# Three PSUM banks for turned blocks in a shared-key attention, and where eight broadcast matmuls stand

## The chip, the cores and the metric

The kernel runs on one core of one Trainium2 chip. The metric is the time of one execution in microseconds on that core. An engine of the core works through its own queue in order: PE is the matrix engine (TensorE), DVE is VectorE, ACT is ScalarE, POOL is GpSimd, SP is the queue that issues most transfers. They wait for each other through semaphores. PE writes its results to PSUM, which has 8 banks of 128 x 512 f32, and ACT or DVE copy them out.

## The reference, cut to what matters

One transformer block for 1024 tokens of width 1024: adaLN from a conditioning vector, two attention branches side by side, a gated merge, and a mixture of experts.

```
mod = silu(c) @ w_mod + b_mod            # 6 x 1024 values
sh1, sc1, gt1, sh2, sc2, gt2 = split(mod, 6)
h = modulate(rmsnorm(x, g_mix), sh1, sc1)
x = x + gt1 * token_mixers(h)            # branches A and B
h = modulate(rmsnorm(x, g_ffn), sh2, sc2)
x = x + gt2 * hier_moe(h);  out = rmsnorm(x, g_final)
```

Branch B is attention with 8 heads of 64 and a bias of forget gates. Branch A is attention with 8 query heads of 64 and **one** key and value head, on 256 keys that an indexer chooses for each query. Both are causal over blocks of 128 tokens.

## The kernel before, in words

**Units.** The attention is cut into 64 units, `UNITS[n]`. A unit is a pair of heads and a query block `b` of 128 tokens, so it has b+1 key blocks. Units 0 to 31 (`N_B` = 32) are branch B, four pairs with b from 7 down to 0. Units 32 to 63 are branch A, four pairs with b in the order 7, 0, 6, 1, 5, 2, 4, 3. Loops on PE, ACT and DVE run over n from -3 to 63, all in step (`LEAD` = 3). In this text, step n of branch A does this:

- PE: `scores(n+3)` (called S here, L1120) writes the logits of unit n+3 to banks 0 to 3. It waits for `lg_done`, that is for DVE's pass over the unit before. Then for each group f of two key blocks `turn_p(n, f)` (T, L1131) transposes the probabilities of both heads into bank 4 or 5 in turn, and `values(n, f-1)` (V, L1145) multiplies the group before with the values into bank 6. The last V of the unit closes the step. T waits until ACT has copied the group two before; V waits until ACT has copied its own group, and the first V of a unit waits for `o_done`, DVE's copy of the unit before out of bank 6.
- DVE: `out_a(n-1)` (L1619, that copy), `inverse(n+2)` (L1607), `scaled(n+2)` (L1614, the rows divided by their sums, after which the unit may be turned), `largest(n+3)` (L1600, the pass over the logits: bias, row maximum), and then what `parts[n]` has for this step.
- ACT: `turned(n, f)` (L823, the copy of each turned group to SBUF), then `exps(n+3)` (L810, one for each of the two heads).

A unit of width W has W = 128(b+1) logits a row.

**The eight steps before branch A.** In steps 24 to 31, PE also makes the queries of branch A: `qa_tile(i)` (L1159, i = n-24, 16 matmuls into bank 7), which ACT copies out (L829), DVE rotates (`rope_a`, L1648 to L1651) and PE turns one step later (`qa_turn`, L1167). In these steps DVE also runs the search for the 256 keys and, from step 28 on, `choose` (L1635 to L1639), one long piece a step. From step 30 on DVE's order is rope_a, inverse, scaled, largest, and then `parts[n]`; S of step 30 belongs to unit 33.

**The modulation.** For gt1, sh2, sc2 and gt2, DVE sums eight weighted rows of w_mod in each partition (`mod_sums`, L1379 and seven times L1381 for each of eight halves of 512 columns) while PE makes the first projections (L1015, L1020). Later `modulate(n)` multiplies `ones` with such a half on PE (L1176, into bank 7), which adds over the partitions and leaves the sum in all of them, and DVE adds the broadcast rows of b_mod (`bmb`) and writes it back (L1664). It stands in steps 44 to 51 (`MOD_AT` = 44), between the T's and the last V. `modulate_a2` (L1668) follows in step 51; SP loads the first weights of the next stage (L523 to L526) after it.

**Behind the attention.** From step 56 on ACT and DVE also split the activations into two parts (`high`, L843, and `low`, L1672), and the gate stage on PE begins at L1211.

Of the kernel before, what the change touches and what calls it, by code (L numbers as in the profile page):

```python
# [18 lines left out]
P = 128  # L19
# [58 lines left out]
CHOOSE_AT = {28: 7, 29: 6, 30: 5, 31: 2, 32: 4, 33: 3}  # L78
MOD_AT = N_B + TT + 4

# [14 lines left out]
def qa_turn_at(i):  # L95

    return TURN_AT[N_B - TT + 2 + i] - 1


# [23 lines left out]
def build(nc, x, c, positions, w_mod, b_mod, g_mix, w_in, b_forget, w_out_a, w_out_b, w_out, g_ffn,  # L123
# [11 lines left out]
    with ExitStack() as ctx:  # L135
# [105 lines left out]

        bmb = at(8, 4 * U, [4, D])
        gffn = at(12, U)
# [216 lines left out]
        def _(sp):  # L460
# [15 lines left out]
            sp.wait_ge(modp_ok, 1)  # L476
            for n in range(4, 12):
                if n >= 6:
                    sp.wait_ge(acc_ok, n - 3)
                sp.dma_start(mod2[n % 2], w_mod_v[:, :, n * 512:(n + 1) * 512]).then_inc(mod_in[n % 2], 16)  # L480
# [36 lines left out]
            sp.wait_ge(qa_ps, TT)  # L517
            for q in range(4):
                sp.dma_start(bmb[:, q, :], b_mod[0:1, (2 + q) * D:(3 + q) * D].to_broadcast([P, D])).then_inc(bmb_in, 16)
            sp.dma_start(gffn, g_ffn[0:1, :].to_broadcast([P, D])).then_inc(bmb_in, 16)  # L520
# [82 lines left out]
        def _(pool):  # L603
# [19 lines left out]
            pool.wait_ge(p_in, 64)  # L623
            pool.wait_ge(consts, 3)

            for t in range(TT):
# [91 lines left out]
        def _(act):  # L718
# [99 lines left out]
            def turned(n, f):  # L818
                g, k, keys = GROUP_AT[n] + f, TURN_AT[n] + f, key_groups(n)[f]
                act.wait_ge(t_done, k + 1)  # L820
                if g >= 4:
                    act.wait_ge(pv_done, g - 3)
                act.activation(pT_of(n, g)[:, 0:2 * len(keys) * P], ps[:, 4 + k % 2, 0:2 * len(keys) * P], ACT.Copy).then_inc(pt_copied, 1)  # L823

# [143 lines left out]
        def _(pe):  # L968
# [154 lines left out]
            def turn_p(n, f):  # L1123
                k, keys = TURN_AT[n] + f, key_groups(n)[f]
                if f == 0:
                    pe.wait_ge(n_done, 2 * n + 2)
                if k >= 2:
                    pe.wait_ge(pt_copied, k - 1)
                for i, kb in enumerate(keys):
                    for z in range(2):  # L1130
                        m = pe.transpose(ps[:, 4 + k % 2, (2 * i + z) * P:(2 * i + z + 1) * P], logits(n)[z][:, kb * P:(kb + 1) * P], ident[:])  # L1131
                m.then_inc(t_done, 1)
# [18 lines left out]
            def qa_tile(i):  # L1151
                t = TILES[i]
                if i == 0:
                    pe.wait_ge(wqa_in, 64)
                    pe.wait_ge(pj_out, 6 * PAIRS)
                else:
                    pe.wait_ge(qa_tm, i)
                for kt in range(KT):
# [11 lines left out]
            def modulate(n):  # L1170
                if n == 0:
                    pe.wait_ge(acc_ok, 10)
                    pe.wait_ge(qa_tm, TT)
                else:
                    pe.wait_ge(mbc_ok, n)
                pe.matmul(ps[:, 7, :], ones[:], acc[2 + n // 2][:, (n % 2) * 512:(n % 2 + 1) * 512], start=True, stop=True).then_inc(mbc_ps, 1)  # L1176

            for n in range(-LEAD, N_U):
                if n + LEAD < N_U:
                    scores(n + LEAD)  # L1180
                groups = len(key_groups(n)) if n >= 0 else 0
                for f in range(groups):
                    turn_p(n, f)
# [8 lines left out]
                elif N_B - TT <= n < N_B:  # L1192
                    qa_tile(n - (N_B - TT))
                elif MOD_AT <= n < MOD_AT + 8:
                    modulate(n - MOD_AT)
                if groups:
                    values(n, groups - 1)
            pe.wait_ge(mbc_ok, 9)
            pe.wait_ge(o_done, N_U)
# [167 lines left out]
        def _(dve):  # L1367
# [6 lines left out]
            def mod_sums(n):  # L1374
# [3 lines left out]
                a = acc[n // 2][:, (n % 2) * 512:(n % 2 + 1) * 512]  # L1378
                link(dve.tensor_scalar(a, w[:, 0, :], sil[:, 0:1], None, ALU.mult))  # L1379
                for t in range(1, KT):  # L1380
                    m = dve.scalar_tensor_tensor(a, w[:, t, :], sil[:, t:t + 1], a, ALU.mult, ALU.add)  # L1381
# [277 lines left out]
            def modulate(n):  # L1659
                if n == 0:  # L1660
                    dve.wait_ge(bmb_in, 96)
                half = slice((n % 2) * 512, (n % 2 + 1) * 512)
                dve.wait_ge(mbc_ps, n + 1)
                dve.tensor_tensor(acc[2 + n // 2][:, half], ps[:, 7, :], bmb[:, n // 2, half], ALU.add).then_inc(mbc_ok, 1)  # L1664

            def modulate_a2():
                dve.wait_ge(mbc_ok, 8)
                dve.scalar_tensor_tensor(a2, a2, 1.0, gffn, ALU.add, ALU.mult).then_inc(mbc_ok, 1)  # L1668
# [9 lines left out]

            for n in range(MOD_AT, MOD_AT + 8):
                parts.setdefault(n, []).append(lambda n=n: modulate(n - MOD_AT))  # L1680
            parts[MOD_AT + 7].append(modulate_a2)
            for n in range(N_U - TT + 1, N_U):
                parts.setdefault(n, []).append(lambda n=n: low(n - (N_U - TT) - 1))

            for n in range(-LEAD, N_U):
                todo = parts.get(n, [])
                if n > N_B:
                    out_a(n - 1)
                if N_B - TT < n <= N_B:
                    rope_a(n - (N_B - TT) - 1)  # L1690
                if N_B <= n + LEAD - 1 < N_U:
                    inverse(n + LEAD - 1)
                    scaled(n + LEAD - 1)
                if n + LEAD < N_U:
                    largest(n + LEAD)
# [250 lines left out]
```

## Time and the profile before

| | |
|---|---|
| median of 3 runs | 1812.57 us (1811.67 to 1814.99) |
| the profiled execution | 1821.39 us, its span 1819.3 us |
| PE busy | 1678.1 us, 92% of the span |
| DVE, ACT, POOL busy | 961.7, 496.6, 191.5 us |
| mean granted TensorE clock | 0.970 of full |
| steps 24 to 31 of the attention | about 466 to 556.6 us of the span |
| branch A, to the first matmul of the gate stage | about 562.7 to 704.7 us |

The span is the time from the first to the last instruction. Line numbers are those of the kernel before. A line of a timeline is a run of one engine's instructions; in brackets stands how long the engine was idle before it and for whom it waited. PEld is the load of weights into the array, which overlaps PE. Durations are those of this one execution.

### The profile page before, as it was taken

Reading aid. Unit: us, or ns where it says so; the run is one execution under the profiler, and the core shown is the slowest. Engines: PE = TensorE matmul, PEld = TensorE weight load, DVE = VectorE, ACT = ScalarE, POOL = GpSimd, SP = SyncE. Lnnn points to the kernel's source line nnn. Section 1 sums busy time; section 2 is a strip of 40 time slices with the busy share of each in tenths; the row PEclk is TensorE's granted clock in tenths of the full one; section 3 lists DMA queues with packets and bytes.
Section 4 is the critical chain, followed back from the end, with each engine's and each line's share of the span. In section 5 each row is a group of like instructions: output and inputs, shape, how many; then the busy total and the mean of one; then the engine's idle time right before and its main releaser. Section 6 shows DMA issues by size and latency. Waiting matters only on the chain.

```text
span 1819.3 us, 22907 instructions
## 1 busy us (share of the span) xinstructions
PE 1678.1 (92%) x7928; PEld 857.8 (47%) x7929; DVE 961.7 (53%) x1913; ACT 496.6 (27%) x1020; POOL 191.5 (11%) x371
## 2 busy tenths in 40 slices
PE   6998899999998998999999998499999989999892
PEld 3553456465545555666676455233333333333330
DVE  6675788787887664655555433533333333333323
ACT  4124455353535564110100111011111111111112
POOL 0110000000000000000000000122222212222221
PEclk9999999999999999999999998699999999999996
DMA  9641201100001020122112713889999747999997
GB/s 358 223 155 59 70 24 48 31 29 1 1 1 59 1 70 1 35 52 51 35 35 108 300 59 133 335 334 398 365 339 398 278 127 237 397 401 367 398 398 253
DMA packets 102906, 316.63 MB, mean 174 GB/s; under 512 B 9921, under 2 KB 46825, under 8 KB 78257
## 3 DMA queue, kind: packets, MB, share of 16 engines
q1 hardware_dynamic: 91088, 287.88, 41.3%
q0 software_dynamic: 11744, 27.79, 6.3%
q8 instruction: 44, 0.72, 0.2%
q14 instruction: 30, 0.24, 0.0%
HBM read 289.14 MB, written 26.51 MB: 173 GB/s over the span
## 4 chain that ended last, share of the span: by engine, by line
PE 82%; ACT 5%; DMA 5%; DVE 4%; issue 2%; SPq 1%; POOLq 0%; DVEq 0%; ACTq 0%
PE ps L1296 18%; PE ps L1222 10%; PE ps L1314 9%; PE ps L1211 6%; PE ps L1095 5%; PE ps L1257 5%; PE ps L1120 4%; PE ps L1145 4%; DMA arena<-in_w_e_up_dram 3%; PE ps L1101 3%; PE ps L1015 3%; PE ps L1159 3%; PE ps L1131 2%; ACT arena L823 2%; PE ps L1053 2%
## 5 line engine op out<-in xcount | busy, mean ns | idle before, releaser
L1296 PE MATMUL ps<-arena 128*64 128x512 f32 x1632 | 376.3, 604 | 19.6 <-issue 14.0
L1296 PEld LDWEIGHTS ps<-arena 128*64 128x64 f32 x1632 | 115.5, 138 | 233.4 <-issue 219.5
L1884 DVE COPY arena<-ps 128x256 f32<-128x256 f32 x51 | 21.7, 425 | 383.6 <-ACT arena L931 383.6
L1314 PE MATMUL ps<-arena 128*64 128x512 f32 x816 | 186.4, 599 | 0.6 <-DVE arena L1906 0.6
L1222 PE MATMUL ps<-rounded 128*128 128x512 f32 x768 | 183.3, 398 | 0.0
L1535 DVE TENSOR_SCALAR_CACHE_REDUCE arena<-arena,small 128x384 bf16<-128x384 f32 (+2 forms) x192 | 171.1, 939 | 0.0
L1222 PEld LDWEIGHTS ps<-rounded 128*128 128x128 f32 x768 | 144.3, 188 | 36.5 <-issue 7.7
L710 POOL DMA_INDIRECT sum_rows<-arena,ones x51 | 81.4, 1595 | 434.9 <-DVE arena L1906 424.0
L1145 PE MATMUL ps<-arena 128*64 128x128 f32 x1152 | 96.4, 286 | 23.1 <-ACT arena L823 21.5
L1211 PE MATMUL ps<-arena 128*128 128x512 f32 x256 | 115.6, 606 | 2.2 <-DVEq L1708 2.2
L1257 PE MATMUL ps<-arena 128*128 128x512 f32 x256 | 112.0, 595 | 2.0 <-DMA arena<-in_w_out_dram 2.0
L935 ACT ACTIVATE arena<-ps 128x256 f32<-128x256 f32 x51 | 19.5, 383 | 340.8 <-PE ps L1305 340.8
L1600 DVE CUSTOM_DVE_ANT_0 arena<-ps,arena 128x896 f32<-128x896 f32 (+7 forms) x128 | 91.7, 754 | 36.9 <-PE ps L1120 34.8
L823 ACT ACTIVATE arena<-ps 128x512 f32<-128x512 f32 (+1 forms) x160 | 85.4, 551 | 88.3 <-PE ps L1131 88.2
L1714 DVE RECIPROCAL arena<-arena 128x1024 f32<-128x1024 f32 x16 | 104.8, 6553 | 0.5
L810 ACT ACTIVATE arena<-arena,small 128x896 f32<-128x896 f32 (+7 forms) x128 | 97.8, 768 | 10.0 <-DVE small L1600 9.9
L1314 PEld LDWEIGHTS ps<-arena 128*64 128x64 f32 x816 | 54.2, 136 | 94.0 <-issue 88.0
L1145 PEld LDWEIGHTS ps<-arena 128*64 128x64 f32 x1152 | 59.7, 136 | 70.9 <-ACT arena L823 45.3
L1131 PE MATMUL ps<-ident,arena 128*128 128x128 f32 x576 | 89.1, 287 | 0.0
L1889 DVE RECIPROCAL arena<-arena 128x256 f32<-128x256 f32 x51 | 89.1, 1746 | 0.0
L1120 PE MATMUL ps<-arena 64*128 64x512 f32 (+3 forms) x384 | 80.9, 527 | 7.8 <-DVE small L1600 6.9
L890 ACT ACTIVATE arena<-ps 128x1024 f32<-128x1024 f32 x16 | 16.4, 1023 | 259.1 <-PE ps L1222 259.1
(297 smaller groups left out, 2013.7 us busy)
## 6 DMA issues: line engine op xcount, KB each, us to landing
arena<-in_w_e_gate_dram SPq DMA_DIRECT2D x64, 1024.0 KB, 16.5
arena<-in_w_e_up_dram SPq DMA_DIRECT2D x64, 1024.0 KB, 19.1
arena<-in_w_e_down_dram SPq DMA_DIRECT2D x32, 2048.0 KB, 15.8
arena<-in_w_mod_dram SPq DMA_DIRECT2D x12, 2048.0 KB, 9.6
arena<-in_w_in_dram SPq DMA_DIRECT2D x32, 512.0 KB, 4.4
arena<-in_x_dram SPq DMA_DIRECT2D x16, 512.0 KB, 8.3
sum_rows<-arena SPq DMA_DIRECT2D x9, 512.0 KB, 2.6
arena<-cum_rows SPq DMA_DIRECT2D x8, 512.0 KB, 5.3
```

Of the source, the lines that this page charges most:

```text
L810: act.activation(buf, buf, ACT.Exp, bias=nmax[:, u:u + 1], scale=-1.0, accum_out=rs[:, u:u + 1]).then_inc(p_done, 1)
L823: act.activation(pT_of(n, g)[:, 0:2 * len(keys) * P], ps[:, 4 + k % 2, 0:2 * len(keys) * P], ACT.Copy).then_inc(pt_copied, 1)
L1120: m = pe.matmul(ps[:, 2 * z + a // 512, 0:e - a], q[half, b * P:(b + 1) * P], k[half, a:e], start=True, stop=True)
L1131: m = pe.transpose(ps[:, 4 + k % 2, (2 * i + z) * P:(2 * i + z + 1) * P], logits(n)[z][:, kb * P:(kb + 1) * P], ident[:])
L1145: m = pe.matmul(ps[z * HD:(z + 1) * HD, 6, 0:P], v, pT_of(n, g)[:, (2 * i + z) * P:(2 * i + z + 1) * P], start=kb == 0, stop=kb == b)
L1211: m = pe.matmul(ps[:, 4 * half + 2 + g, :], w[2 + g][:, kt, :], oT[g][kt][:, tok], start=kt == 0, stop=kt == 3)
L1222: m = pe.matmul(ps[:, 4 * half + g, :], a, b, start=kt == 0 and k == 0, stop=kt == KT - 1 and k == 2)
L1257: m = pe.matmul(ps[:, 2 * (t % 2) + n, :], mT[:, kt, t * P:(t + 1) * P], wout[:, kt, n * 512:(n + 1) * 512], start=kt == 0, stop=kt == KT - 1)
L1296: m = pe.matmul(ps[o * TB:(o + 1) * TB, 2, 0:2 * FQ].rearrange("p (j n) -> p j n", j=2), xT[:, k % NX, k // NX * TB:(k // NX + 1) * TB], w ...
L1314: m = pe.matmul(ps[o * TB:(o + 1) * TB, 5, 0:DQ], hidT[:, k % NH_T, k // NH_T * TB:(k // NH_T + 1) * TB], w_dn[c][:, k, o * DQ:(o + 1) * D ...
L1535: chain.up(dve.tensor_scalar(junk[b % 2][:, 0:WB[B0 + b]], scb[b], thr(b), None, op, ALU.add, accum_out=cnt[:, b:b + 1]))
L1714: link(dve.reciprocal(e, e))
```

## The change

It has three parts.

1. In branch A from unit 33 on (`FIRST_OF_THREE`), turned groups go through banks 7, 4 and 5 (or 7, 5, 4) in turn, and V runs two groups behind T. The last V of a unit moves behind the S of the next step. T waits for the copy three groups before. DVE's `out_a(n-1)` moves from the head of the step to behind `scaled(n+2)`, in front of `largest(n+3)`.
2. Bank 7 must therefore be free by then: the eight `modulate` move from steps 44 to 51 to steps 24 to 31, between S and the first T on PE and at the head of `parts[n]` on DVE. They share bank 7 with qa_tile: `modulate(i)` waits until ACT has copied tile i-1, and `qa_tile(i)` waits for DVE's copy of half i (`mbc_ok`). `modulate_a2` stands in step 44, and so do the weights that wait for it.
3. b_mod is in the sums from the start: POOL clears four 1024-column tiles (`at(45, 4 * U)`), SP loads the row of b_mod into partition 0 of them, and `mod_sums` adds to that, so that its first instruction is a scalar_tensor_tensor too. The four broadcasts of b_mod fall away, and DVE's part of `modulate` becomes a copy.

```diff
@@ the order of banks
-MOD_AT = N_B + TT + 4
+MOD_AT = N_B - TT
+A2_AT = N_B + TT + 4
+FIRST_OF_THREE = N_B + 1
+def turn_bank(k):
+    k -= TURN_AT[FIRST_OF_THREE]
+    return (7, 4 + TURN_AT[FIRST_OF_THREE] % 2, 5 - TURN_AT[FIRST_OF_THREE] % 2)[k % 3] if k >= 0 else 4 + (k + TURN_AT[FIRST_OF_THREE]) % 2
+def copied_before(k):
+    since = k - TURN_AT[FIRST_OF_THREE]
+    return k - 1 if since < 0 else k - 2 if since else 0
@@ SP, loads for the modulation
             for n in range(4, 12):
+                if n == 6:
+                    sp.wait_ge(consts, 4)
+                    sp.dma_start(at(45, 4 * U)[0:1, :], b_mod[0:1, 2 * D:6 * D]).then_inc(c_in, 16)
...
-            for q in range(4):
-                sp.dma_start(bmb[:, q, :], b_mod[0:1, (2 + q) * D:(3 + q) * D].to_broadcast([P, D])).then_inc(bmb_in, 16)
             sp.dma_start(gffn, g_ffn[0:1, :].to_broadcast([P, D])).then_inc(bmb_in, 16)
@@ POOL
+            pool.wait_ge(ssq_ok, TT)
+            pool.wait_ge(modp_ok, 1)
+            pool.memset(at(45, 4 * U), 0.0).then_inc(consts, 1)
@@ PE, turn_p, qa_tile and modulate
-                    pe.wait_ge(pt_copied, k - 1)
+                    pe.wait_ge(pt_copied, copied_before(k))
...
-                    pe.wait_ge(pj_out, 6 * PAIRS)
-                else:
-                    pe.wait_ge(qa_tm, i)
+                pe.wait_ge(mbc_ok, i + 1)
...
-                    pe.wait_ge(qa_tm, TT)
+                    pe.wait_ge(pj_out, 6 * PAIRS)
                 else:
-                    pe.wait_ge(mbc_ok, n)
+                    pe.wait_ge(qa_tm, n)
@@ PE, the loop
-            for n in range(-LEAD, N_U):
-                if n + LEAD < N_U:
-                    scores(n + LEAD)
+            for n in range(-LEAD, FIRST_OF_THREE):
+                scores(n + LEAD)
                 groups = len(key_groups(n)) if n >= 0 else 0
+                if MOD_AT <= n < MOD_AT + 8:
+                    modulate(n - MOD_AT)
                 for f in range(groups):
                     turn_p(n, f)
                     if f >= 1:
...
-                elif MOD_AT <= n < MOD_AT + 8:
-                    modulate(n - MOD_AT)
                 if groups:
                     values(n, groups - 1)
+            for n in range(FIRST_OF_THREE, N_U):
+                if n + LEAD < N_U:
+                    scores(n + LEAD)
+                if n > FIRST_OF_THREE:
+                    values(n - 1, len(key_groups(n - 1)) - 1)
+                groups = len(key_groups(n))
+                for f in range(groups):
+                    turn_p(n, f)
+                    if f >= 2:
+                        values(n, f - 2)
+                if groups >= 2:
+                    values(n, groups - 2)
+            values(N_U - 1, len(key_groups(N_U - 1)) - 1)
@@ DVE, mod_sums
-                link(dve.tensor_scalar(a, w[:, 0, :], sil[:, 0:1], None, ALU.mult))
-                for t in range(1, KT):
+                if n == 4:
+                    dve.wait_ge(c_in, 32)
+                for t in range(KT):
                     m = dve.scalar_tensor_tensor(a, w[:, t, :], sil[:, t:t + 1], a, ALU.mult, ALU.add)
@@ DVE, modulate
-                dve.tensor_tensor(acc[2 + n // 2][:, half], ps[:, 7, :], bmb[:, n // 2, half], ALU.add).then_inc(mbc_ok, 1)
+                dve.tensor_copy(acc[2 + n // 2][:, half], ps[:, 7, :]).then_inc(mbc_ok, 1)
...
-                parts.setdefault(n, []).append(lambda n=n: modulate(n - MOD_AT))
-            parts[MOD_AT + 7].append(modulate_a2)
+                parts.setdefault(n, []).insert(0, lambda n=n: modulate(n - MOD_AT))
+            parts.setdefault(A2_AT, []).append(modulate_a2)
@@ DVE, the loop
-                if n > N_B:
+                if N_B < n <= FIRST_OF_THREE:
                     out_a(n - 1)
...
                     scaled(n + LEAD - 1)
+                if n > FIRST_OF_THREE:
+                    out_a(n - 1)
                 if n + LEAD < N_U:
                     largest(n + LEAD)
```

## Rows read from the trace of the kernel before

**Rows 1.** The page: the chain that ended last, shares by engine.

```profile
PE 82%; ACT 5%; DMA 5%; DVE 4%; issue 2%; SPq 1%; POOLq 0%; DVEq 0%; ACTq 0%
```

**Rows 2.** Windows: steps 24 to 31, and branch A with the step before.

```profile
471.00:562.00 91.00, 88.81 (x420) 45.16 (x416) 73.43 (x185) 37.41 (x93) 2.20 (x8) 1.00 0.00 1
562.00:704.70 142.70, 123.94 (x1011) 74.55 (x1009) 100.16 (x258) 92.93 (x204) 0.00 (x0) 0.99 0.15 42
```

**Rows 3.** Waits in 562 to 704.7 us: total, times, longest.

```profile
PEld ps L1145 <- ACT arena L823: 22.0, 36, 1.6
...
PE ps L1145 <- ACT arena L823: 11.2, 28, 1.4
```

**Rows 4.** The chain that ended last, step 44: start, length.

```profile
616.92 1.06 PE ps L1176 x2
617.97 0.59 PE ps L1145 x8
```

**Rows 5.** Timeline of PE, steps 30 and 31: start, length.

```profile
539.32 7.03 PE L1159 MATMUL ps<-arena 128*128 128x512 f32 x16
...
549.29 7.03 PE L1159 MATMUL ps<-arena 128*128 128x512 f32 x16
```

**Rows 6.** Timeline of DVE: the ends of `largest` in steps 30 and 31.

```profile
540.63 0.08 DVE L1600 DVE_READ_ACCUMULATOR2_ANT small<- 128x1 f32 x1
...
550.72 0.08 DVE L1600 DVE_READ_ACCUMULATOR2_ANT small<- 128x1 f32 x1
```

**Rows 7.** Groups by line: busy us, mean ns, idle before.

```profile
L823 ACT ACTIVATE arena<-ps 128x512 f32<-128x512 f32 (+1 forms) x160 | 85.4, 551 | 88.3 <-PE ps L1131 88.2
...
L1403 DVE COPY arena<-ps 128x512 f32<-128x512 f32 x8 | 5.5, 686 | 1.4 <-PE ps L981 1.4
```

**Rows 8.** Timeline of ACT: second exps of the 512-wide units 39, 47, 55, 63.

```profile
582.66 0.71 ACT L810 ACTIVATE arena<-arena,small 128x512 f32<-128x512 f32 x1
...
617.56 0.71 ACT L810 ACTIVATE arena<-arena,small 128x512 f32<-128x512 f32 x1
...
658.38 0.71 ACT L810 ACTIVATE arena<-arena,small 128x512 f32<-128x512 f32 x1
...
693.66 0.71 ACT L810 ACTIVATE arena<-arena,small 128x512 f32<-128x512 f32 x1
```

**Rows 9.** Timeline, steps 38 and 41, PE, DVE and ACT.

```profile
588.67 1.42 DVE L1614 TENSOR_SCALAR arena<-arena,small 128x1024 f32<-128x1024 f32 x2
...
600.64 1.56 PE L1120 MATMUL ps<-arena 64*128 64x512 f32 x8
...
600.79 0.19 ACT L810 ACTIVATION_READ_ACCUMULATOR arena<-arena,small 128x1 f32 x1
...
601.21 0.62 DVE L1614 TENSOR_SCALAR arena<-arena,small 128x256 f32<-128x256 f32 x2
...
602.25 0.96 DVE L1600 CUSTOM_DVE_ANT_0 arena<-ps,arena 128x768 f32<-128x768 f32 x1 [0.42 <-PE ps L1120]
...
603.25 0.94 ACT L810 ACTIVATE arena<-arena,small 128x768 f32<-128x768 f32 x1 [0.26 <-DVE small L1600]
```

**Rows 10.** Groups by line: DVE's sums for the modulation, POOL's memset.

```profile
L1381 DVE SCALAR_TENSOR_TENSOR arena<-arena,small 128x512 f32<-128x512 f32 x56 | 42.1, 752 | 2.0
...
L1379 DVE TENSOR_SCALAR arena<-arena,small 128x512 f32<-128x512 f32 x8 | 3.8, 480 | 0.0
...
L616 POOL MEMSET ones<- 128x128 f32 x1 | 0.3, 264 | 0.0
```

**Rows 11.** Timeline of DVE and PEld in the first projections, with idle time before.

```profile
42.13 3.71 DVE L1443 TENSOR_SCALAR arena<-arena,small 128x1024 f32<-128x1024 f32 x5
...
44.44 0.34 PEld L1015 LDWEIGHTS ps<-arena 128*128 128x128 f32 x1 [0.52 <-DVE arena L1443]
...
76.99 0.33 DVE L1477 TENSOR_TENSOR arena<-arena,small 128x128 f32<-128x128 f32 x1 [2.91 <-ACT arena L766]
...
143.26 0.23 DVE L1518 COPY small<-ps 128x64 f32<-128x64 f32 x1 [4.43 <-PE ps L1080]
```

More of the change, by code:

```diff
@@ L239, in build @@
         qaT = [at(u, 2 * U, [2, S]) for u in (21, 27)]
-        bmb = at(8, 4 * U, [4, D])
         gffn = at(12, U)
@@ L822, in turned @@
                     act.wait_ge(pv_done, g - 3)
-                act.activation(pT_of(n, g)[:, 0:2 * len(keys) * P], ps[:, 4 + k % 2, 0:2 * len(keys) * P], ACT.Copy).then_inc(pt_copied, 1)
+                act.activation(pT_of(n, g)[:, 0:2 * len(keys) * P], ps[:, turn_bank(k), 0:2 * len(keys) * P], ACT.Copy).then_inc(pt_copied, 1)
             def qa_copy(i):
@@ L1127, in turn_p @@
                 if k >= 2:
-                    pe.wait_ge(pt_copied, k - 1)
+                    pe.wait_ge(pt_copied, copied_before(k))
                 for i, kb in enumerate(keys):
                     for z in range(2):
-                        m = pe.transpose(ps[:, 4 + k % 2, (2 * i + z) * P:(2 * i + z + 1) * P], logits(n)[z][:, kb * P:(kb + 1) * P], ident[:])
+                        m = pe.transpose(ps[:, turn_bank(k), (2 * i + z) * P:(2 * i + z + 1) * P], logits(n)[z][:, kb * P:(kb + 1) * P], ident[:])
                 m.then_inc(t_done, 1)
@@ L1659, in modulate @@
             def modulate(n):
-                if n == 0:
-                    dve.wait_ge(bmb_in, 96)
                 half = slice((n % 2) * 512, (n % 2 + 1) * 512)
                 dve.wait_ge(mbc_ps, n + 1)
-                dve.tensor_tensor(acc[2 + n // 2][:, half], ps[:, 7, :], bmb[:, n // 2, half], ALU.add).then_inc(mbc_ok, 1)
+                dve.tensor_copy(acc[2 + n // 2][:, half], ps[:, 7, :]).then_inc(mbc_ok, 1)
             def modulate_a2():
+                dve.wait_ge(bmb_in, 32)
                 dve.wait_ge(mbc_ok, 8)
```

## The prediction

> **What bounds the kernel now.** I read the chain of waits first. PE holds 82% of it [rows 1], so a change pays where PE waits and costs where PE is full. The windows then divide the stretch that the change touches [rows 2]. In steps 24 to 31 PE is busy 88.81 of 91.00 us: whatever is put into its queue there is paid. In branch A it is busy 123.94 of 142.70, DVE 100.16, ACT 92.93: no engine is full, and the engines wait for each other in turn. Last the waits of branch A: V's weight loads waited 22.0 us in 36 places for ACT's copies of turned groups, its matmuls 11.2 us in 28 [rows 3]; the two overlap, so they are not added. The change aims at these. What follows branch A starts when it ends, so a gain or loss there reaches the end undiminished.
>
> **The modulates arrive in steps 24 to 31.** One on the chain takes 1.06 us, the change of operation behind it included [rows 4]. Between S and the first T of a step PE has no gap before. Steps 24 to 29 therefore pay 6 x 1.05 = 6.3 us. DVE's copy (0.69 us, the like of L1403, [rows 7]) comes behind `largest`, while PE still turns and multiplies, so qa_tile does not wait for it in these six.
>
> Steps 30 and 31 differ: DVE has scaled and largest of branch A ahead of it. In step 30 largest frees DVE at 540.63; the copy ends at 541.32 and PE sees it at 541.37. Before, qa_tile started at 539.32 [rows 5, 6]. That is 2.05 us, and the 1.05 of the matmul lies inside. In step 31 it is 550.72 + 0.69 + 0.05 = 551.46 against 549.29 [rows 5, 6], 2.17 us. Sum for the pair in front: 6.3 + 2.05 + 2.17 = **+10.5**. Below: if half of the six matmuls hid behind copies, +7.4. Above: if DVE's search pieces pushed two more copies onto the path like step 30, +12.5.
>
> **They leave branch A.** The second exps of units 39, 47, 55 and 63 stand 34.90, 40.82 and 35.28 us apart [rows 8]. The middle eight steps hold modulates and a2, the others almost none. Their stay costs 40.82 - 34.90 = 5.9 us, less than 8 x 1.06, since they cover part of a copy that V waits for.
>
> **The three banks.** With T's two ahead, V waits less. But two orders change too, and both can cost. I worked the eight kinds of steps (n mod 8) through, always with the same rules. Time zero is the end of the exps of the step before. A group of T or V takes 0.43 us, and 0.16 more where PE changes from one operation to another (0.59 in all, [rows 4]). ACT's copy takes 0.55 [rows 7]. On DVE come inverse and out_a (0.2 each), scaled and largest. The exps start when the first half of largest and the last copy of the unit are both done.
>
> Step 41 (n mod 8 = 1) as an example. Before, S started at 600.64, the exps of the step before ended at 600.79 + 0.19 = 600.98, and largest waited for S until 602.25, which is 1.27 after time zero; the exps followed at 603.25 [rows 9]. After, the turns finish earlier and S starts at -0.60 instead of -0.34, ends at 0.68, and the deferred V runs from 0.84 to 1.27. It is visible at 1.43, out_a takes 0.2, and largest starts at 1.66. The step becomes 4.6 us long instead of 4.2, although scaled (0.62, [rows 9]) was done long before. What is late there is largest, behind out_a, behind a V that stands behind S.
>
> The second cost: the first V of a unit needs out_a. Behind scaled of a 1024-wide unit (1.42 us, [rows 9]) out_a ends near 1.85, V starts near 2.0, and the next S and its copies slip; the 896-wide step grows by 0.6. The gain falls to steps 2 and 4 (units with many groups), 0.65 and 0.47. The table gives step lengths in us; those before are from the sixteen exps between the first two of [rows 8].
>
> | n mod 8 | 5 | 6 | 7 | 0 | 1 | 2 | 3 | 4 | sum |
> |---|---|---|---|---|---|---|---|---|---|
> | before | 4.98 | 2.77 | 5.16 | 4.60 | 4.23 | 4.95 | 3.49 | 4.72 | 34.9 |
> | after | 5.20 | 2.97 | 5.73 | 4.54 | 4.60 | 4.30 | 3.90 | 4.25 | 35.5 |
>
> So the banks by themselves give nothing: +0.6 a pair of heads. Steps 37 to 44: +0.6. Steps 45 to 52: 35.5, and 0.4 for a2, which now lengthens DVE in step 44: 35.9 - 40.8 = -4.9. Steps 53 to 60: 35.5 + 0.3 for low on DVE, against 35.28: +0.5. The steps before and after (33 to 36, 61 to 63), by the same rule, -0.8. Branch A: **-4.6**. Bounds: if nothing of the reordering cost and every V wait counted for PE's loads went, the 22.0 of [rows 3] would be gained beside the modulates; nearer is the loop of ACT and DVE without V's waits, about 32 a pair (exps, inverse, scaled, out_a, largest, one behind the other), which gives 3 x 3.5 = 10.5 more than my sum. On the other side, 0.1 us more in each of 28 steps, 3 us. I stay with the table, since both orders that it charges are written into the queues, and with its unit costs, which rows give.
>
> **b_mod in the sums.** Eight first instructions become 752 - 480 = 272 ns longer [rows 10], 2.2 us of DVE. Each is hidden: DVE idles 2.91 us before the next tile's rope, and 4.43 before PE has the sums of the forget gates [rows 11]. Without that cover it would be 2.2. The row of b_mod is 16 KB on SP's queue, issued where SP would wait for DVE anyway. The four broadcasts and their transfers lay beside branch A and held nothing up. POOL's memset is the open cost: no row shows one of 4096 columns. From 264 ns for 128 [rows 10], 32 x 0.264 = 8.4 us is the most; three such memsets start 0.14 us apart, so an estimate is 32 x 0.14 = 4.5. It begins with DVE's L1443 at about 42 and ends near 46.5, and only mod_sums, from 58 on, needs it. I take 0, with up to 6.6 above (below).
>
> **The sum.** +10.5 - 4.6 + 0 = +5.9. The durations are of an execution of 1821.39 us (span 1819.3, and 2.1 around it), 8.8 above the median of 1812.57; a difference of 5.9 carries over, and gives **1818.5 us**.
>
> **The rivals.**
>
> *The banks earn.* If out_a and the deferred V are not late as I have them, steps fall to the loop of about 32 and 10.5 us more are saved: +5.9 - 10.5 = -4.6, **1808.0**, faster. For it: 36 waits for one producer [rows 3]. Against it: DVE's order, and PE's. It decides if largest in step 41 starts by 1.3 us after the exps. The Trainium skill speaks for it (Perfetto Trace Analysis, Optimization Strategy): a gap that repeats on the engine that should be full can mean that buffers ran out. By that rule the third bank would fill the gaps; the trace agrees that the gap repeats, but by my table most of it is the loop.
>
> *They cancel.* Half of that gain, or modulates in steps 24 to 29 half hidden: +5.9 - 5.3 = +0.6, or +2.8; about **1814**, no change that can be measured.
>
> *POOL's memset holds DVE.* Both start once modp_ok is there. If the memset bars DVE's L1443 until it ends, the second weight load of the first projection, now at 44.44 and already waiting for that line [rows 11], goes to 46.3 + 0.74 = 47.1, +2.6 (at 8.4 us for the memset, +6.6). With the forecast +8.5, **1821**. For it: L1443 does 1024 columns in 0.74 us (3.71 / 5), twice the pace of L1381's 512 in 0.75 [rows 10, 11]. The Trainium skill (SBUF — State Buffer, two separate sides) has such a rule: GpSimd and a VectorE operation in a two-port mode exclude each other for a whole instruction. No row of this trace has the two together.
>
> **Chances.** Forecast 0.42, cancel 0.24, banks earn 0.16, memset 0.18. A difference under 0.2%, 3.6 us, is about what a measurement cannot tell from none. The forecast and the memset case are slower nearly always (0.57 with the edge of the second case), the cancelling one mostly the same (0.27), the banks faster (0.16). Range 1809 to 1823: it leaves out the far side of the banks' case and the memset at its longest. The forecast's own range is 1815 to 1821.
>
> **What would show it.** In the trace after: steps 24 to 29 each 1.05 us longer; qa_tile waiting for DVE's copy of bank 7 in steps 30 and 31 by 1.0 us; V's waits for L823 mostly gone, and waits for L1619 in their place; L1600 waiting for PE's V; eight steps of branch A near 35.5. Wrong it would be if the eight steps took 32, if modulates lay in gaps, or if L1443 stood still beside POOL.

## The result, and the profile after

| | before | after |
|---|---|---|
| median | 1813.78 us (4 runs, 1811.67 to 1817.94) | 1833.93 us (4 runs, 1829.46 to 1839.6) |
| ratio | | 1.0105, 95% interval 1.008 to 1.0129 |
| span of the profiled execution | 1819.3 us | 1837.8 us |

The change makes the kernel slower by 1.0%. The profiled execution is the slowest of its four, 5.7 us above their median; two losses below belong to it alone.

The page of the changed kernel, the chain that ended last, shares by engine:

```profile
PE 82%; DVE 6%; DMA 4%; ACT 3%; issue 2%; SPq 2%; POOLq 0%; DVEq 0%; ACTq 0%
```

PE holds as much as before, but DVE now has 6% where it had 4, and ACT 3% where it had 5 [rows 1]. What came onto the path is work of DVE that PE waits for.

**The head.** Timeline of the changed kernel, first projection: start, length, and in brackets the idle time before and for whom. Line numbers are now those of the changed kernel (L1473 was L1443, L1034 was L1015). A run that stands last in a view is cut off at the view's end: the x8 here is 16 matmuls long, and so is the x7 of the last qa_tile below.

```profile
43.50 3.51 POOL L643 MEMSET arena<- 128x4096 f32 x1 [41.10 <-PE ps L1021]
...
43.87 6.58 DVE L1473 TENSOR_SCALAR arena<-arena,small 128x1024 f32<-128x1024 f32 x5
...
45.16 1.13 PE L1034 MATMUL ps<-arena 128*128 128x512 f32 x2 [1.80 <-ACT arena L767]
...
47.62 9.17 PE L1034 MATMUL ps<-arena 128*128 128x512 f32 x14 [1.33 <-DVE arena L1473]
...
56.62 1.57 PE L1039 MATMUL ps<-arena 128*128 128x208 f32 x8
```

DVE's five scalings took 3.71 us before [rows 11] and take 6.58 with the memset beside them. Only the first of the five is long, 3.69 us for 0.81; the other four take 0.80 each, as before. PE's third matmul waits for them. The first 16 matmuls last from 45.16 to 56.62, where the next run starts: 11.46 us, against 9.55 in the trace before. The scalings also began 1.74 us later than before (42.13, [rows 11]), since a slice of w_mod landed later (DVE waited 3.89 us for it, 2.33 before). The edit does not touch that slice, and the start of the scalings differs as much between executions of code that is alike there (the last section).

**Steps 27 to 31.** Timeline of DVE and of PE in the changed kernel:

```profile
512.07 0.69 DVE L1692 COPY arena<-ps 128x512 f32<-128x512 f32 x1
517.09 0.17 DVE L1637 RECIPROCAL small<-small 128x2 f32<-128x2 f32 x1 [4.33 <-ACT arena L829]
...
517.35 3.07 DVE L1656 TENSOR_SCALAR arena<-arena,small 128x384 f32<-128x384 f32 x6
```

```profile
526.92 0.66 PE L1184 MATMUL ps<-ident,arena 128*128 128x128 f32 x4 [1.04 <-DVE arena L1681]
527.95 8.80 PE L1176 MATMUL ps<-arena 128*128 128x512 f32 x16 [0.36 <-DVE arena L1692]
...
553.77 7.13 PE L1176 MATMUL ps<-arena 128*128 128x512 f32 x16 [1.51 <-DVE arena L1692]
...
566.01 3.27 PE L1176 MATMUL ps<-arena 128*128 128x512 f32 x7 [1.10 <-DVE arena L1692]
```

The last two lines answer to [rows 5]: qa_tile waits for DVE's copy of the modulate in steps 30 and 31. The first two are new: in step 27 DVE stands idle for 4.33 us with the sign change (L1656) still to do, the rotation of tile 3 is late by as much as PE has no other work for (1.04 and 0.36 us), and the qa_tile behind takes 8.80 us, not 7.03. Before, the last qa_tile started at 549.29; now at 566.01, 16.7 later.

**Branch A.** Timeline of ACT, second exps of units 39, 47, 55 and 63, as [rows 8]:

```profile
601.11 0.73 ACT L829 ACTIVATE arena<-arena,small 128x512 f32<-128x512 f32 x1
...
637.33 0.73 ACT L829 ACTIVATE arena<-arena,small 128x512 f32<-128x512 f32 x1
...
675.02 0.73 ACT L829 ACTIVATE arena<-arena,small 128x512 f32<-128x512 f32 x1
...
712.71 0.73 ACT L829 ACTIVATE arena<-arena,small 128x512 f32<-128x512 f32 x1
```

They stand 36.22, 37.69 and 37.69 us apart, against 34.90, 40.82 and 35.28. Waits of the changed kernel in 579 to 723.2 us: total, times, longest:

```profile
PE ps L1139 <- DVE small L1630: 17.0, 14, 2.7
...
PEld ps L1164 <- ACT arena L842: 13.1, 22, 1.6
...
DVE arena L1649 <- PE ps L1164: 10.6, 12, 1.5
PE ps L1164 <- DVE arena L1649: 7.2, 7, 2.5
...
PE ps L1164 <- ACT arena L842: 3.8, 8, 1.4
```

The wait that the banks aimed at fell: V's loads for copies, from 22.0 us in 36 places [rows 3] to 13.1 in 22, V's matmuls for copies from 11.2 in 28 to 3.8 in 8. Two others grew more: S waits 17.0 us for `largest` (4.1 in 6 places before), and V 7.2 us for out_a (0.6 before).

**The clock.** Windows of the changed kernel in the second pair: length, then busy time of PE, PEld, DVE, ACT and POOL, the granted clock, and the DMA's share and GB/s:

```profile
658.60:661.00 2.40, 0.62 (x4) 0.38 (x6) 2.04 (x5) 1.59 (x4) 0.00 (x0) 1.00 0.00 0
661.00:664.40 3.40, 3.40 (x17) 2.09 (x14) 2.46 (x8) 1.34 (x3) 0.00 (x0) 0.51 0.00 0
664.40:668.40 4.00, 4.00 (x43) 2.73 (x41) 0.75 (x3) 2.66 (x7) 0.00 (x0) 0.99 0.02 6
```

After 2.4 us in which PE was busy 0.62, it is granted half its clock (1.2 of 2.4 GHz) for 3.4 us. Two timelines of PE show the same instructions in the pair before and in this one:

```profile
624.48 0.92 PE L1139 MATMUL ps<-arena 64*128 64x384 f32 x4 [1.78 <-DVE small L1630]
625.33 0.44 PE L1164 MATMUL ps<-arena 128*64 128x128 f32 x4
625.70 1.53 PE L1150 MATMUL ps<-ident,arena 128*128 128x128 f32 x12
...
660.70 1.35 PE L1139 MATMUL ps<-arena 64*128 64x384 f32 x4 [1.78 <-DVE small L1630]
661.98 0.70 PE L1164 MATMUL ps<-arena 128*64 128x128 f32 x4
662.60 2.41 PE L1150 MATMUL ps<-ident,arena 128*128 128x128 f32 x12
```

The wait of 1.78 us is the same; only behind the second did the clock fall, and the pair is 1.47 us longer (37.69 - 36.22). The undisturbed pair of the changed kernel is thus 36.22 us. The long qa_tile of step 28 (8.80 us) is such a stretch too: the mean granted clock over it is 0.81.

### The profile page after: what moved, and what is told of

It reads as the page before. It is cut to its first block, busy times and chain, and to the rows that moved or that the text cites. A ratio compares the mean times of both kernels' runs of the same rounds, so it can differ in the third digit from the quotient of the medians.

```text
span 1837.8 us, 22905 instructions
## 1 busy us (share of the span) xinstructions
PE 1677.8 (91%) x7928; PEld 860.5 (47%) x7929; DVE 965.6 (53%) x1913; ACT 496.3 (27%) x1020; POOL 194.8 (11%) x372
## 4 chain that ended last, share of the span: by engine, by line
PE 82%; DVE 6%; DMA 4%; ACT 3%; issue 2%; SPq 2%; POOLq 0%; DVEq 0%; ACTq 0%
PE ps L1325 19%; PE ps L1251 9%; PE ps L1343 9%; PE ps L1240 6%; PE ps L1114 5%; PE ps L1286 5%; PE ps L1139 4%; PE ps L1164 4%; PE ps L1120 3%; PE ps L1034 3%; PE ps L1176 3%; PE ps L1150 2%; PE ps L1072 2%; PE ps L1319 2%; DVE arena L1630 2%
```

## The experiments

Each kernel ran beside the kernel before on the same chip, in two rounds of four kernels and one of two; the kernel before gave 1818.59, 1818.46 and 1815.77 us there, so ratios are compared rather than medians.

**e0: the changed kernel again.** No edit.

> The changed kernel once more, unaltered, on the chip of these runs, as the measure for e2 and e3, whose differences of 2 us are small beside what parts one execution from another: by its first timing the ratio to the kernel before is 1.0105, some 19 us. Its trace is to show which of the losses come back in a second execution: the five scalings at 6.6 us, the idle stretch of VectorE in step 27, the units 36.2 us apart or 37.7 with a stretch of lower granted clock in each pair; and which don't: the lower clock at the eighth part of step 28 (the projection of 8.8 us), which is expected to be gone.

1832.73 us (6 runs), ratio 1.009, interval 1.0073 to 1.0106. The pairs stand 36.22, 37.68 and 37.69 us apart again, and the idle stretch of step 27 came back, but the projection of step 28 took its normal length (7.13 us). Between the exps of units 24 and 34 it needs 115.8 us (117.5 in the first execution, 105.6 before): 1.7 us of the first trace were that one stretch of low clock.

**e2: the memset later.**

```
-            pool.wait_ge(modp_ok, 1)
+            pool.wait_ge(sin_ok, 1)
             pool.memset(at(45, 4 * U), 0.0).then_inc(consts, 1)
```

> The changed kernel with GpSimd's clearing of the 128x4096 tile held back until the sines are done, when VectorE has an idle stretch of 6.5 us. Theory (the clearing held VectorE): the five scalings of 128x1024 take 3.7 us again and not 6.58, TensorE's first projection ends about 1.9 us earlier beside the second-last of the modulation sums, the time falls by 1.9 to about 1832 us. Rival (those five were slow for another reason, for instance ScalarE's work beside them): they stay at 6.5 us and the time stays.

1829.83 us, ratio 1.007 (1.0054 to 1.0085), against 1.009 of e0. The timeline of e2:

```profile
43.42 3.71 DVE L1473 TENSOR_SCALAR arena<-arena,small 128x1024 f32<-128x1024 f32 x5
...
44.72 8.83 PE L1034 MATMUL ps<-arena 128*128 128x512 f32 x16 [1.81 <-ACT arena L767]
...
50.12 3.51 POOL L643 MEMSET arena<- 128x4096 f32 x1 [47.71 <-ACT small L770]
50.15 0.23 DVE L1492 TENSOR_TENSOR small<-small 128x64 f32<-128x64 f32 x1 [0.48 <-ACT small L770]
...
50.41 3.27 DVE L1493 TENSOR_SCALAR small<-small 128x64 f32<-128x64 f32 x1
50.52 3.20 DVE L1494 TENSOR_SCALAR small<-small 128x64 f32<-128x64 f32 x1
...
53.38 2.98 PE L1039 MATMUL ps<-arena 128*128 128x208 f32 x16
```

The scalings take 3.71 us again, with ScalarE's passes (3.51 us) still beside them, so the rival falls: the memset held DVE. It still does where it now stands. Two scalings of only 64 columns take 3.27 and 3.20 us beside it, 0.20 and 0.19 in the kernel before, but DVE has nothing on the path to do there.

What the memset costs is less sure. The ratio gives some 3.6 us with an uncertainty as large. The first 16 matmuls take 8.66 us instead of 11.46, but part of that is where the half clock of the start ends: over all twelve traces they take 10.09 to 11.46 us with the memset beside the scalings (seven traces) and 8.65 to 9.88 without (five), 1.4 us apart in the mean. The Trainium skill has the rule (SBUF — State Buffer, two separate sides): GpSimd and a VectorE instruction in a two-port mode exclude each other for the whole instruction. The trace of the changed kernel agrees within 0.3 us: the memset of 3.51 us had started 0.37 us before the scalings, and they ended 2.87 us late, where the rule makes 3.14.

**e3: the split of DVE's list as before.**

```
-                half = len(todo) // 2 if n + LEAD < N_B else 0
+                moved = int(MOD_AT <= n < MOD_AT + 8)
+                half = moved + (len(todo) - moved) // 2 if n + LEAD < N_B else 0
```

> The changed kernel with VectorE's list of pieces split as before the change, the modulate not counted: in step 27 the sign change runs ahead of the reciprocal again, while the exponentials are still under way. Theory (the shifted split left VectorE idle for 4.3 us in step 27 and made the rotation of tile 3 late): the wait of 1.04 us ahead of the turning of tile 3 and the 0.36 us ahead of the next projection are gone, and steps 24 to 31 take 1.4 us less; 3.2 us less, where the slow projection of 8.8 us in step 28 comes from that wait too. Time 1831 to 1833 us. Rival (another wait of the step takes the place): steps 24 to 31 stay within 0.5 us.

1829.63 us, ratio 1.0067 (1.0048 to 1.0086). Between the exps of units 24 and 34 it needs 114.1 us, 1.7 less than e0. The timeline of DVE in e3:

```profile
510.27 3.07 DVE L1656 TENSOR_SCALAR arena<-arena,small 128x384 f32<-128x384 f32 x6
514.56 0.17 DVE L1637 RECIPROCAL small<-small 128x2 f32<-128x2 f32 x1 [1.22 <-ACT arena L829]
```

The sign change fills the wait for the exps again, of which 1.22 us is left where 4.33 was; neither qa_turn nor qa_tile of step 28 waits for DVE. The split cost 1.7 us, not the 3.2 of the expectation's upper case: the low clock behind it came only in the first execution and is absent from e0 as well.

**e1: two banks, values one behind, the modulates stay moved.** The loops of steps 33 to 63 on PE and DVE as before the change, and `turn_bank` always 4 or 5.

> The changed kernel with its attention part put back for steps 33 to 63: two banks in turn, the values one group behind, the unit's last values in its own step, the copy of the output first on VectorE; the modulates stay in steps 24 to 31. Theory A (the new order costs): the stretch from the last projection of steps 24 to 31 to the start of the gate stage was 155.4 us in the kernel before, with 5.9 us for the modulates in it, and 157.2 us after. It comes to 149 to 151 us, the four units 39, 47, 55, 63 stand about 35 us apart (after: 36.2, 37.7, 37.7), and the time is 1834 - 7 = 1827 us. Theory B (the modulates' leaving gave nothing, for instance because the granted clock falls): the stretch stays at 155 to 158 us and the time at 1832 to 1836 us.

1826.23 us, ratio 1.0049 (1.0033 to 1.0065). The second exps start at 596.57, 631.47, 666.37 and 701.65: 34.90, 34.90 and 35.28 apart. Timeline of ACT in e1, the middle pair:

```profile
631.47 0.71 ACT L829 ACTIVATE arena<-arena,small 128x512 f32<-128x512 f32 x1
...
666.37 0.71 ACT L829 ACTIVATE arena<-arena,small 128x512 f32<-128x512 f32 x1
```

The middle pair, 40.82 with the modulates in it, has become 34.90: their stay cost 5.9. From the start of the last qa_tile to the gate stage e1 needs 149.6 us (157.2 in the changed kernel, 155.4 before), as theory A has it. The third bank with the new order costs 1.3 us a pair, and 1.5 more where the clock falls, which it does not in e1's pairs.

**e4: three banks, two behind, last values in their own step.**

```
-                if n > FIRST_OF_THREE:
-                    values(n - 1, len(key_groups(n - 1)) - 1)
...
                 if groups >= 2:
                     values(n, groups - 2)
-            values(N_U - 1, len(key_groups(N_U - 1)) - 1)
+                values(n, groups - 1)
```

and on DVE `out_a(n - 1)` first in every step from 33 on.

> The changed kernel with three banks and values two groups behind, but each unit's last values again at the end of its own step and the copy of the output first on VectorE. Theory A1 (what costs is the delaying of the last values past the next scores, which then wait for VectorE's copy of the output, now behind the scaling): the stretch of steps 33 to 63 comes to 149 to 151 us and the time to about 1827 us. Theory A2 (the distance of two groups costs by itself, since the turned blocks of a unit are all made before its values and the unit ends later): it stays at 155 us or more, time 1832 to 1836 us.

1813.03 us (12 runs), ratio 0.9975 (0.9961 to 0.9988). Timeline of ACT in e4, second exps of the same four units:

```profile
594.32 0.73 ACT L829 ACTIVATE arena<-arena,small 128x512 f32<-128x512 f32 x1
...
626.24 0.73 ACT L829 ACTIVATE arena<-arena,small 128x512 f32<-128x512 f32 x1
...
658.16 0.73 ACT L829 ACTIVATE arena<-arena,small 128x512 f32<-128x512 f32 x1
...
690.36 0.73 ACT L829 ACTIVATE arena<-arena,small 128x512 f32<-128x512 f32 x1
```

31.92, 31.92 and 32.20 us: not near the 35 of two banks, as A1's 1827 us implied, but 3 us a pair below them; A1 had the cause in part and the size wrong, and A2 is refuted. The third bank and the distance earn together, and what spoiled them is what e4 takes back. Waits of e4 in 572 to 700 us:

```profile
PEld ps L1164 <- ACT arena L842: 16.8, 35, 1.6
...
DVE arena L1647 <- PE ps L1164: 11.9, 17, 1.2
...
PE ps L1139 <- DVE small L1628: 5.4, 10, 1.8
```

S's wait for `largest` is down from 17.0 to 5.4 us. V's loads wait in 35 places, more often than in the changed kernel, and the pair is 4.3 us shorter: that wait was no measure of the gain.

**e8 and e9: the two halves of the order.** e4 took back two things; e8 puts out_a behind scaled again, with the last values in their own step, and e9 keeps the last values behind the next scores and puts out_a first. e9's edit, on the changed kernel:

```
-                if N_B < n <= FIRST_OF_THREE:
+                if n > N_B:
                     out_a(n - 1)
...
-                if n > FIRST_OF_THREE:
-                    out_a(n - 1)
```

> The kernel of e4 (three banks, values two groups behind, each unit's last values in its own step) with one thing of the change back: VectorE copies the output of the unit before after the scaling, not first. e4 has its units 39, 47, 55, 63 31.9 us apart, the changed kernel 36.2 to 37.7, of which about 1.5 each is a stretch of 3.4 us at the lower granted clock. Theory C (what cost was the last values behind the next scores: TensorE meets the wait for the row maxima with nothing left to do): stays at 32 to 33 us, ratio to the kernel before about 0.998. Theory D (what cost was the copy of the output behind the scaling, which keeps the next unit's first values waiting): 35 to 37 us, ratio about 1.007.

> The changed kernel, last values still behind the next unit's scores, but VectorE copies the output of the unit before first in its step, ahead of the scaling. Theory C: the four units stay 35 to 37.7 us apart, as in the changed kernel, ratio about 1.01. Theory D: they come to 32 to 33 us, ratio about 0.998. Were it both, each by a half, this one and e8 would both stand near 34.

e8: 1826.9 us, ratio 1.0057 (1.0037 to 1.0076); second exps at 595.27, 630.00, 664.72 and 699.49. e9: 1847.22 us, ratio 1.0167 (1.0143 to 1.019); at 597.64, 638.71, 679.78 and 720.80. The pair from unit 39 to unit 47:

| three banks, values two behind | out_a first | out_a behind scaled |
|---|---|---|
| last values in their own step | 31.92 (e4) | 34.72 (e8) |
| last values behind the next scores | 41.07 (e9) | 36.22 (changed) |

Neither C nor D alone, and they do not add. With the values in their own step, out_a behind scaled costs 2.8 us by itself. Waits of e8 in 572 to 700 us:

```profile
PE ps L1164 <- DVE arena L1647: 12.0, 10, 2.9
```

With out_a first, the deferred values cost 9.2: DVE's copy then waits for values that stand behind scores, and all of DVE's step behind it. The timeline of DVE in e9 and its waits in 572 to 720 us:

```profile
613.44 0.29 DVE L1649 COPY arena<-ps 128x128 f32<-128x128 f32 x1 [1.39 <-PE ps L1164]
613.64 0.15 DVE L1637 RECIPROCAL small<-small 128x2 f32<-128x2 f32 x1
613.84 1.28 DVE L1644 TENSOR_SCALAR arena<-arena,small 128x896 f32<-128x896 f32 x2
```

```profile
DVE arena L1649 <- PE ps L1164: 59.1, 26, 4.2
...
PE ps L1139 <- DVE small L1630: 27.3, 14, 2.7
```

Once the values are deferred, out_a has to go behind scaled, and the changed kernel is the better of the two bad cases. Deferring costs wherever out_a stands, 9.2 us or 1.5 (36.22 - 34.72). But it is not the whole mistake: of the 4.3 us a pair that the changed kernel loses against e4, e8 has 2.8 without any deferring. Of e9's 9.2 us about 3 are the clock, an estimate: the pair has two stretches of low clock, at 1.47 us each as above, and the mean granted over it is 0.92.

**e10: the kernel before, two banks, only the order of the values.**

```
+                behind = 2 if n > N_B else 1
                 for f in range(groups):
                     turn_p(n, f)
-                    if f >= 1:
-                        values(n, f - 1)
+                    if f >= behind:
+                        values(n, f - behind)
+                if behind == 2 and groups >= 2:
+                    values(n, groups - 2)
```

> The kernel before, with two banks, the modulates in steps 44 to 51 as they were and b_mod by its broadcasts, and one edit: in steps 33 to 63 the values run two groups behind, the last ones still in their own step. Theory E (the order alone earns what e4 earned; a third bank adds nothing, since the values two behind wait for the same copy as the turning that two banks hold back): the undisturbed pairs go from 34.9 and 35.3 us to about 32, the ratio to the kernel before is 0.993 to 0.996, below e4's 0.9975, as the ten us that the moved modulates cost in steps 24 to 31 are not paid. Theory F (the third bank is what earns): the pairs stay at 34.5 to 35.3 us and the ratio at 1.000.

1810.74 us (9 runs), ratio 0.9963 (0.995 to 0.9976). The second exps start at 581.49, 614.84, 655.04 and 688.79: 33.35, 40.20 and 33.75 us apart. Timeline of ACT in e10, the first pair:

```profile
581.49 0.71 ACT L810 ACTIVATE arena<-arena,small 128x512 f32<-128x512 f32 x1
...
614.84 0.71 ACT L810 ACTIVATE arena<-arena,small 128x512 f32<-128x512 f32 x1
```

The order alone earns 1.55 us of the 2.98 that order and third bank earn together; both theories have half. A third bank with the values one group behind was not run, so what it earns without the distance stays open. Against e4 no difference can be told, since the intervals overlap. In the traces e10 saves 10.2 us from unit 24 to 34 (105.6 for 115.8), where it has no modulates, and loses 10.3 from unit 34 to 63 (137.4 for 127.2), where it has them and only two banks.

**e11: b_mod in the sums, alone.** e10 with the row of b_mod in the sums, the broadcasts gone, DVE copying instead of adding, the memset as in e2; the modulates in steps 44 to 51.

> The kernel of e10 (two banks, values two groups behind, modulates in steps 44 to 51) with b_mod as the changed kernel has it: the row loaded once into a cleared tile and taken up in the sums, no broadcasts, VectorE copying instead of adding; the clearing held back as in e2. Theory (b_mod in the sums costs and gives nothing once the clearing is out of the way): within 0.1% of e10's ratio of 0.9963. Rival 1 (the copy is cheaper than the addition and the bank comes free earlier in steps 44 to 51): the pair with the modulates falls from 40.2 us by 0.5 or more. Rival 2 (the first of the eight sums, now a multiply-add, or its wait for the row, holds the projections' rotations): 0.3 to 1 us slower ahead of unit 0.

1810.3 us (12 runs), ratio 0.9975 (0.996 to 0.999), beside 0.9963. That is 0.12% off where the expectation had 0.1%, 2.2 us, and each interval alone is some 2.5 us wide either way, so no difference can be told. The pair with the modulates stays at 40.20, so rival 1 falls. Rival 2's 0.3 to 1 us is too small for these runs: from the scalings to the exps of unit 0 e11 needs 171.3 us and e10 175.0, but e7, with the code of e11 up to there, 175.3. e11 is granted the full clock at 128 to 140 us, where e10 and e7 have a stretch at half. No cost and no gain of b_mod in the sums is shown.

**e7: the repairs together.** e4, e2 and e3, and the copies of modulates 6 and 7 ahead of `largest`:

```
+                if N_B - 2 <= n < N_B:
+                    todo.pop(0)()
                 if n + LEAD < N_U:
                     largest(n + LEAD)
```

> All that the runs so far point to, on the changed kernel: three banks and values two groups behind with each unit's last values in its own step and the copy of the output first (e4), the clearing held back (e2), the split without the modulate (e3), and, new here, VectorE's copies of modulates 6 and 7 in steps 30 and 31 ahead of the row maxima, not behind them. Theory: the losses are separate and add. Against e4: 2 to 2.7 us by the clearing, 1.7 us by the split, and 1.5 to 2.5 us of the stalls of 1.51 and 1.10 us ahead of the last two projections; 1813 - 6 = 1807 us, ratio to the kernel before 0.994; the stretch from the exponentials of unit 24 to those of unit 34 takes 112 us (115.8 in e4, 105.6 before). Rival (the copy ahead delays the row maxima by as much, since the matmul of the modulate only comes behind the scores): the stretch takes 114 us, 1809 us.

1807.59 us (7 runs), ratio 0.9953 (0.9933 to 0.9974): 8.5 us faster than the kernel before, the fastest here, though its interval meets those of e10, e11 and e4. The time meets the 1807 that was expected, but partly because the kernel before was 2.8 us faster there than beside e4. By the ratios e7 is 4.0 us faster than e4 (0.9953 against 0.9975), not 6. The timeline of PE in e7:

```profile
546.92 7.13 PE L1176 MATMUL ps<-arena 128*128 128x512 f32 x16 [1.09 <-DVE arena L1690]
...
558.19 7.13 PE L1176 MATMUL ps<-arena 128*128 128x512 f32 x16
```

The wait in step 31 is gone, that of step 30 fell from 1.51 to 1.09. Exps of units 24 to 34 take 114.2 us, as in the rival; but 1.4 us more comes behind unit 34, since qa_tile 7 ends earlier. Measured from the exps of unit 24 to those of unit 40, e7 needs 148.4 us and e4 151.5: 3.2 us, 1.7 of it the split and the rest the copies, the lower end of what the theory gives for the two.

## Why the prediction was wrong

It forecast 1818.5 us and a range of 1809 to 1823; 1833.93 was measured. The direction was right, and for a reason that it gave: the modulates are paid in full in steps 24 to 31. The spans of the two profiles lie 18.5 us apart where it had +5.9. What failed above all is the term of the banks: branch A without the modulates was to grow by 1.3 us, and it grew by 7.6 (157.2 us from the last qa_tile to the gate stage, 149.6 in e1), about 4.4 of it by stretches of low clock that the sum did not have. The other errors, the split and the memset, go the same way, so nothing cancelled. By its own steps:

- **Steps 24 to 29, 6 x 1.05.** Mis-sized a little: each undisturbed step grew by 0.90 to 0.92 us (the first qa_tile starts at 475.66, not 471.19; 3.56 of that was there by the end of the last projections, at 461.41 for 457.85; the next three steps likewise, and step 29 in e7). 5.5, not 6.3.
- **Steps 30 and 31, 2.05 and 2.17.** Right: 2.05 and 2.27, with qa_tile waiting 1.51 and 1.10 for the copy. The working took the starts in [rows 6] for ends; with the 0.08 us that each row lasts it gives 2.13 and 2.25, as near.
- **Missed: the split.** The prediction took DVE's search pieces to stay where they were. DVE runs the first `half` of a step's list ahead of `inverse`, and `half` counts the modulate put at the head of the list. In step 27 the list has two pieces in the kernel before and three in the changed one, half is 1 in both, and so the sign change slipped behind `inverse`. 1.7 us, shown by e3. The first trace has 1.77 more in qa_tile of step 28 from the clock, which e0 does not have. In all 13.2 where +10.5 stood; without the clock, 11.4.
- **The modulates leave branch A, 5.9.** Right: e1's middle pair is 34.90.
- **The banks, +0.6 a pair.** This failed, in two ways. The first is the size. As a reckoning of this order the table was close, but most of its steps a little short: its eight steps are 5.29, 2.97, 5.95, 4.71, 4.68, 4.37, 3.90 and 4.35 in the trace, 36.22 in all where it had 35.5, so +1.3 and not +0.6. Step 41 went as described: in the first pair the deferred V starts 0.84 us after time zero and `largest` at 1.75, where it had 0.84 and 1.66.
- **The clock, not in the sum.** The second is that the table took the full clock as given. In the pairs of steps 45 to 52 and 53 to 60 the clock fell behind a wait of PE, 1.47 us each. Ahead of unit 39 a stretch of low clock costs about 1.5 more (from the exps of unit 34 to those of unit 39 e0 needs 34.6 us, and e3, where it comes earlier, 33.1); the kernel before has a low clock near there too, at 566 to 571 us. So the three pairs came out at +1.3, -3.1 and +2.4, against +0.6, -4.9 and +0.5. From the exps of unit 34 to those of unit 63 it takes 3.6 us more, not 4.6 less; 1.4 of the 3.6 is the late last qa_tile, which stands there in e1 too.
- **The reading of it, "the banks by themselves give nothing".** The sum was near, the sentence false. The third bank and the distance earn 2.98 us a pair (e4, 31.92 us, near the loop of about 32 that the rival "banks earn" named), and the order loses 4.3 again (changed against e4). The prediction named both costly orders, the deferred values and out_a behind scaled, but charged them as one with the banks. So it could not say that bank and distance earn, nor that each order costs by itself (e8, e9). Its sign "V's waits for L823 mostly gone" did not come either: the loads still wait 13.1 us of 22.0, the matmuls 3.8 of 11.2. The waits in their place came (V for out_a, 7.2 us).
- **b_mod in the sums, 0.** Not contradicted (e11), but the runs would not show a cost under some 3 us.
- **The memset, 0 taken, 2.6 as a rival.** The rival was true: the wait of PE's load for the scalings came as it described. The memset took 3.51 us, less than the estimate of 4.5, and cost 1.9 us in the first trace and 1.4 in the mean of all. It had been given 0.18.
- **Outside the change:** 1.7 us of the profiled difference is the later start of the scalings; the medians do not rest on it.

What both executions of the changed kernel share, by the exps: 1.4 to 2 (memset), 10.2 from unit 24 to 34 (115.8 - 105.6), and 3.6 from there to unit 63, 15 to 16 us in all; the ratios 1.009 and 1.0105 give 16 to 19.

## What to carry to other kernels

A deeper ring of buffers earns only if the order of the queue lets the engine run ahead; try depth and order separately, because together they showed only the sum of a gain of 3 us (half of it from the distance alone) and a loss of 4.3 a pair. The last step of a tile must not stand behind the next tile's first instruction when that instruction waits for another engine: whatever releases the tile (here out_a) inherits the wait. The copy that frees the tile must not stand behind a long pass either: that alone cost 2.8 us a pair. And a piece put into a list that is cut by its length moves every other piece: read what the cut does before pricing the piece.

## What the runs showed of the hardware

- GpSimd's memset of 128x4096 f32 took 3.51 us and held the first of five VectorE scalings of 128x1024, which took 3.69 us instead of 0.81; the five took 6.58 instead of 3.71. ScalarE's three passes over like tiles beside them took 3.50, as without the memset. In e2 it held two scalings of 128x64, 3.27 and 3.20 us instead of 0.20 and 0.19, while a TENSOR_TENSOR of 128x64 that started 0.03 us after it by the profile took its usual 0.23.
- A PE wait of 1.78 us that comes once a pair was followed by 3.4 us at half the clock, 1.47 us on the path, in the second and third pair of two executions of the changed kernel and not in the first. In e2 all three pairs had one (37.73, 37.69, 37.69). In e3, whose pairs stand even earlier than e2's, the first was spared again. e4, with the same work, had none from unit 39 to 63. Why the first pair is spared in some executions stays open, and so does what makes the clock fall.
- In the twelve traces, whose code differs little up to there, the first scalings started between 42.1 and 43.9 us, by when w_mod had landed; a comparison of two single profiles carries up to 1.7 us of that. From there to the exps of unit 24 e7 needs 403.3 us and e11, with the same code in that stretch, 399.0: e11 has the full clock at 128 to 140 and at 232 to 240 us, where e7 has stretches at half.
